# S5 data through DRAM in fewer transfers, and attention scores of meta and band keys in one product

## What is computed

```python
u = rmsnorm(h)                       # (528, 1024)
gla = gated_linear_attention(q, k, v, a)                 # chunks of 64, state passed on
y   = s5(u_s)                        # per group of 16 channels one 64-dim complex diagonal state
y   = gelu(y + d_skip * u_s); y = y * sigmoid(y @ w_glu)
s   = q @ keys.T + rel_bias          # keys: 16 meta, the chunk before, the own chunk
p   = exp(s - m) / (sum(exp(s - m)) + exp(sink - m))     # a sink per head
att = p @ vals
h   = h + merge(gates(u), gla, y, att) @ w_out
```

## Time and profile before

| | |
|---|---|
| median of 3 runs | 1917.71 us (1917.54 to 1918.06) |
| the profiled execution, its own time | 1920.78 us |
| its span, first to last instruction | 1919.0 us |
| TensorE busy, mean granted clock | 93%, 0.96 |
| weight loads of TensorE busy | 83% |
| DVE, ACT, POOL busy | 51%, 36%, 41% |
| DMA: moved, mean rate | 221.78 MB, 116 GB/s |

### The profile page before, as it was taken

One profiled execution on the slowest core, in us unless ns is written; L12 is line 12 of the kernel. 1 busy time (PEld: TensorE's weight loads), 2 busy tenths in 40 slices (PEclk: granted clock), 3 DMA queues, 4 the chain that ended last, 5 costly groups with the idle time before them and its releaser, 6 DMA issues.

```text
span 1919.0 us, 29485 instructions
## 1 busy us (share of the span) xinstructions
PE 1778.7 (93%) x12215; PEld 1592.5 (83%) x12215; DVE 969.2 (51%) x1527; ACT 693.9 (36%) x1236; POOL 791.1 (41%) x484
## 2 busy tenths in 40 slices
PE   6976899999998998999997999989999899999997
PEld 5876798999988998999996987777788688778886
DVE  8997125423428994277653222433334589634223
ACT  3443332443543222233333643333445222224232
POOL 2644566333223223433343786653333333244442
PEclk8898899999999998999998999999999999999999
DMA  8455236222254562535552333542222646333432
GB/s 147 136 162 154 76 91 133 73 77 69 65 139 135 181 178 78 105 93 168 170 155 73 110 88 92 114 115 73 66 67 64 191 167 208 90 91 96 144 100 87
DMA packets 357068, 221.78 MB, mean 116 GB/s; under 512 B 50628, under 2 KB 347768, under 8 KB 354376
## 3 DMA queue, kind: packets, MB, share of 16 engines
q1 hardware_dynamic: 346408, 189.75, 37.4%
q10 hardware_dynamic: 10528, 30.15, 4.6%
HBM read 172.17 MB, written 38.50 MB: 110 GB/s over the span
## 4 chain that ended last, share of the span: by engine, by line
PE 65%; DVE 10%; DMA 7%; POOL 7%; ACT 4%; SPq 4%; issue 3%; ACTq 0%; DVEq 0%; POOLq 0%
PE ring L807 47%; DMA sb_w_raw<-in_w_in 4%; POOL sb_w_lo L658 3%; PE ring L766 3%; PE aux L1066 2%; DVE sb_s_mat_prod L1553 2%; PE aux L1158 2%; DVE sb_s_prod L1553 2%; PE ring L788 1%; SPq L564 1%; PE aux L1145 1%; SPq L530 1%; DMA sb_w_raw<-in_w_s_out 1%; PE aux L1111 1%; DVE sb_s_rot L2052 1%
## 5 line engine op out<-in xcount | busy, mean ns | idle before, releaser
L658 POOL TENSOR_TENSOR sb_w_lo<-sb_w_raw,sb_w_hi 128x1024 fp32r<-128x1024 f32 x246 | 608.7, 2477 | 1044.3 <-ACT sb_w_hi L1210 1042.1
L1210 ACT ACTIVATE sb_w_hi<-sb_w_raw 128x1024 fp32r<-128x1024 f32 x246 | 260.1, 1057 | 618.0 <-DMA sb_w_raw<-in_w_in 359.7
L807 PE MATMUL ring<-sb_u_hi,sb_w_hi 128*128 128x264 f32 (+1 forms) x2112 | 366.8, 327 | 29.0 <-DVE sb_tmp_dve L1623 17.6
L807 PEld LDWEIGHTS ring<-sb_u_hi,sb_w_hi 128*128 128x128 f32 x2112 | 312.0, 201 | 61.5 <-DVE sb_tmp_dve L1623 19.3
L807 PE MATMUL ring<-sb_u_lo,sb_w_hi 128*128 128x264 f32 (+1 forms) x2112 | 338.4, 311 | 0.0
L807 PE MATMUL ring<-sb_u_hi,sb_w_lo 128*128 128x264 f32 (+1 forms) x2112 | 334.4, 309 | 0.0
L807 PEld LDWEIGHTS ring<-sb_u_lo,sb_w_hi 128*128 128x128 f32 x2112 | 298.4, 190 | 22.1
L807 PEld LDWEIGHTS ring<-sb_u_hi,sb_w_lo 128*128 128x128 f32 x2112 | 294.0, 188 | 21.0
L1242 ACT ACTIVATE sb_tmp_act<-ring 128x528 f32<-128x528 f32 (+1 forms) x112 | 67.4, 602 | 140.1 <-PE ring L807 131.8
L807 PE MATMUL ring<-sb_y_hi,sb_w_hi 128*128 128x264 f32 (+1 forms) x504 | 88.8, 326 | 3.4 <-ACT sb_w_hi L1210 3.4
L1473 ACT ACTIVATE sb_att_scores<-sb_att_scores,sb_att_neg_max 128x208 f32<-128x208 f32 x128 | 58.5, 458 | 91.5 <-DVE sb_att_neg_max L1841 91.5
(11 more groups left out here) (324 smaller groups left out, 2618.6 us busy)
## 6 DMA issues: line engine op xcount, KB each, us to landing
sb_w_raw<-in_w_in SPq DMA_DIRECT2D x166, 512.0 KB, 4.1
sb_s_loaded<-s_matrices ACTq DMA_DIRECT2D x16, 1808.0 KB, 7.5
s_matrices<-sb_s_phase SPq DMA_DIRECT2D x16, 528.0 KB, 3.2
s_matrices<-sb_s_mbt SPq DMA_DIRECT2D x16, 512.0 KB
s_matrices<-sb_s_ca SPq DMA_DIRECT2D x16, 512.0 KB
sb_w_raw<-in_w_gla_out SPq DMA_DIRECT2D x16, 512.0 KB, 4.1
sb_w_raw<-in_w_attn_out SPq DMA_DIRECT2D x16, 512.0 KB, 4.1
sb_w_raw<-in_s_w_glu SPq DMA_DIRECT2D x16, 512.0 KB, 3.9
```

The source lines that it names most:

```text
L658: pool.tensor_tensor(WL[:, w], WR[:, w], WH[:, w].bitcast(F32), ALU.subtract).then_inc(lo_ready, 1)
L807: last = pe.matmul(RING[:, 2 * r + hf, 0:c1 - c0], w[:, n % SLOTS, kt, :], moving(b[0], xx[:, kt], c0, c1), start=(term == 0 and kt == 0), ...
L1210: act.activation(WH[:, w], WR[:, w], ACT.Copy).then_inc(hi_ready, 1)
```

## The change

Two things. First, S5's input is written tile by tile to a DRAM tensor as soon as each `("sin", j)` block is evacuated, and read back at `("ag", 0)` by 4 transfers in place of 16; each output tile is written to a second DRAM tensor one block after it is made, and read back in three parts of 4 transfers each in place of 16. The last part's split moves from block 22 to block 23. Second, POOL copies the keys once per layer so that each window of meta and band keys lies contiguous, and the scores of a head pair are one product of 208 keys (144 for the first four units, which need no copy).

```diff
-S5_SPLIT = {21: ((0, 4), (4, 6)), 22: ((6, 8),)}
+S5_SPLIT = {21: ((0, 4), (4, 6)), 23: ((6, 8),)}
+SIN_OUT = {min(AT[("sin", j)] + 2, AT[("ag", 0)]): () for j in range(KT)}
+SIN_OUT = {at: tuple(j for j in range(KT) if min(AT[("sin", j)] + 2, AT[("ag", 0)]) == at) for at in SIN_OUT}
...
+        AKX = sb("att_k_windows", [P, 2, ATT_PAIRS - 1, BAND], at=r)
...
+        ZD = nc.dram_tensor("s5_in_rows", [DEPTH, KT, P, STRIDE, STEPS], F32).ap()
+        YD = nc.dram_tensor("s5_out_rows", [DEPTH, KT, P, QUADS, STEPS], F32).ap()
...
+                    if b in SIN_OUT:
+                        for j in SIN_OUT[b]:
+                            evacuated(sp, ly, ("sin", j))
+                            sp.dma_start(ZD[ly, j], Z[:, j]).then_inc(z_spilled, 16)
                     if name == ("ag", 0):
-
-                        evacuated(sp, ly, ("sin", 6), ("sin", 7))
                         sp.wait_ge(h_spilled, 16 * ly + 16)
                         sp.wait_ge(smax_ready, unit(ly, ATT_UNITS - 1))
-                    if name == ("ag", 0):
-                        for q in range(QUADS):
-                            for p in range(STRIDE):
-                                sp.dma_start(Z4[32 * p:32 * p + 32, :, q, :],
-                                             Z[32 * q:32 * q + 32, :, STRIDE - 1 - p, :]).then_inc(
-                                                 steps_loaded, 16)
+                        sp.wait_ge(z_spilled, 16 * KT * (ly + 1))
+                        for p in range(STRIDE):
+                            sp.dma_start(Z4[32 * p:32 * p + 32].rearrange("i j q c -> i (j q) c"),
+                                         ZD[ly, :, :, STRIDE - 1 - p, :].rearrange("j (q i) c -> i (j q) c", q=QUADS)
+                                         ).then_inc(steps_loaded, 16)
+                    if name in S5F and S5F.index(name) - 1 in S5_OUT:
+                        j = S5_OUT[S5F.index(name) - 1]
+                        aux_read(sp, ly, ("y", j))
+                        sp.dma_start(YD[ly, j], Z4[:, j]).then_inc(y_spilled, 16)
                     if name in S5F and S5F.index(name) in S5_YT:
                         j0, j1 = S5_YT[S5F.index(name)]
-                        aux_read(sp, ly, ("y", j1 - 2))
-                        aux_read(sp, ly, ("y", j1 - 1))
+                        sp.wait_ge(y_spilled, 16 * (KT * ly + j1))
                         for q in range(QUADS):
-                            for t in range(STRIDE):
-                                sp.dma_start(YZ[32 * q:32 * q + 32, j0:j1, t, :],
-                                             Z4[32 * t:32 * t + 32, j0:j1, q, :]
-                                             ).then_inc(yt_loaded[YT_PARTS.index((j0, j1))], 16)
+                            sp.dma_start(YZ[32 * q:32 * q + 32, j0:j1].rearrange("i j t c -> i (j t) c"),
+                                         YD[ly, j0:j1, :, q, :].rearrange("j (t i) c -> i (j t) c", t=STRIDE)
+                                         ).then_inc(yt_loaded[YT_PARTS.index((j0, j1))], 16)
...
+                    if b == AT[("av", 0)] + 3:
+                        pool.wait_ge(akd_loaded, 32 * ly + 32)
+                        pool.tensor_copy(AKX[:, :, :, 0:N_META],
+                                         AKD[:, :, 0:N_META].unsqueeze(2).broadcast_to([P, 2, ATT_PAIRS - 1, N_META])
+                                         ).then_inc(windows_ready, 1)
+                        for p in range(1, ATT_PAIRS):
+                            k0 = N_META + P * p - CHUNK
+                            pool.tensor_copy(AKX[:, :, p - 1, N_META:BAND], AKD[:, :, k0:k0 + 3 * CHUNK]
+                                             ).then_inc(windows_ready, 1)
...
-                    k0, nk = (N_META, P) if p == 0 else (q0 - CHUNK, 3 * CHUNK)
                     h = aux_take(ly, ("sc", u))
+                    if p:
+                        pe.wait_ge(windows_ready, ATT_PAIRS * (ly + 1))
                     for h2 in range(2):
-                        for keys, col, n in ((k0, BAND - nk, nk), (0, 0, N_META)):
-                            for a in range(2):
-                                rows = slice(64 * a, 64 * a + 64)
-                                c0 = BAND * h2 + col
-                                last = pe.matmul(AX_[:, 2 * h + a, c0:c0 + n], AQ[rows, 2 * i + h2, q0:q0 + P],
-                                                 AKD[rows, i // 2, keys:keys + n], start=True, stop=True)
+                        for a in range(2):
+                            rows = slice(64 * a, 64 * a + 64)
+                            keys = AKX[rows, i // 2, p - 1, :] if p else AKD[rows, i // 2, 0:N_META + P]
+                            n = BAND if p else N_META + P
+                            last = pe.matmul(AX_[:, 2 * h + a, BAND * h2:BAND * h2 + n], AQ[rows, 2 * i + h2, q0:q0 + P],
+                                             keys, start=True, stop=True)
```

More of the change, by code:

```diff
@@ L615, in _ @@
                     if name == ("mg1", 3):
                         for part in yt_loaded:
-                            sp.wait_ge(part, 256 * ly + 256)
+                            sp.wait_ge(part, 64 * ly + 64)
                         produced(sp, ly, ("glu", KT - 1))
@@ L1138, in step_inputs @@
                     if j == 0:
[L1139 removed]
+                        pe.wait_ge(steps_loaded, 64 * ly + 64)
                     pe.wait_ge(mats_in[j % 2], 16 * (4 * ly + j // 2) + 16)
```

10 lines of the change are left out of this document (5 added, 5 removed).

## The result

| | before | changed |
|---|---|---|
| median | 1917.54 us (1910.10 to 1918.06, 5 runs) | 1901.89 us (1898.04 to 1905.55, 5 runs) |
| ratio | | 0.9926, 95% interval 0.9904 to 0.9947 |
| the profiled execution, its own time | 1920.78 us | 1898.04 us |
| its span | 1919.0 us | 1896.2 us |

The change gains 15.7 us, 0.7%. The forecast was 1888 us, a gain of 29.4: the sign was right, the size half as large, and 1901.9 lies above the range (1871 to 1898).

What follows compares the result with a forecast made beforehand. TensorE was taken to bound the kernel, with 65% of the chain of waits. Scores 13.4 us plus gap B and gap C 16 us made 29.4 us, from 1917.7 to 1888 us; range 1871 to 1898.

Steps and rivals of the forecast that it cites:

- the scores' term: Attention's score products: half the weight loads go, saving 0.42 us per unit, 13.4 us in all (ends 2.9 and 17.6).
- gap A: TensorE's idle time and slow clock at the S5 stage's start, 9.5 and 11.2 us; claimed to stay, gain 0.
- gap B: TensorE's wait for DVE's state of scan 7, late in S5; claimed to go, worth 16 us together with gap C.
- The copy of the keys: Four POOL copies per layer in attention, at most 4.4 us; claimed to cost nothing.
- SP's issues: SP's queue in S5: 4 issues, 2.8 us, per place instead of 16; the new spills' issues claimed to cost nothing.
- rival 1: gap A closes too, because the old gathers held the load back; about 19 us more go, 1869 us; 17%.
- rival 3: gap B or gap C gives way to a new wait; one staying in both layers costs 6 to 10 us; 18%.
- Gap C: TensorE's wait for POOL's low part of ("glu", 0)'s weights, 2.24 us; claimed to go, 16 us together with gap B.
- Rival 4: S5's gathers through DRAM crawl and the load of ("ag", 3) lands late; at 70 KB/us, 1926 us; 4%.

Runs made afterwards that it cites:

- e13: The kernel before without its products of 16 keys; executed once, only score units read: 0.85 us for a later unit, 0.65 for an early one.
- e9: The changed kernel with the gathers of tiles 0 to 5 put ahead of the load of ("ag", 2) in SP's queue; ratio 0.9898 to the kernel before.
- e10: As e9, and the first load of the S5 matrices issued ahead of block ("ag", 0); ratio 0.9885 to the kernel before.
- e11: The changed kernel with one more POOL wait, holding low parts of odd S5F blocks from the ninth until the running scan's state; ratio 0.9890 to the kernel before.
- e14: The kernel before with the new scores and e11's wait, S5's moves as before; ratio 0.9904 to the kernel before.
- e4: The changed kernel with S5's outputs moved as before (16 transfers per part, last split at block 22); ratio 0.9977 to the kernel before.
- e1: The kernel before with the scores' change alone (key copies included), S5's moves as before; ratio 0.9948 to the kernel before.
- e5: The changed kernel run again, with nothing altered; ratio 0.9932 to the kernel before.
- e8: The changed kernel with tiles 0 to 6 gathered before tile 7's spill and the first S5 matrices' load issued before ("ag", 0); ratio 0.9956 to the kernel before.
- e3: The changed kernel with S5's input moved as before (16 transfers from SBUF to SBUF); ratio 0.9922 to the kernel before.
- e12: The kernel before with each product of 16 keys issued twice; executed once, only score units read: 1.65 us for a later unit, 1.45 for an early one.

## Why the prediction was partly right

The measured time lies outside the range: the change is worth half of what I had forecast, because the scores' term was too large, gap A grew where I had put nothing, and gap B came back in another place.

**Scores.** Fewer products make the unit shorter, as forecast; the size was off: 9.7 us for 13.4. The failed step is "I take the narrow pairs as held to the pace of their loads". The rows allowed 0.14 to 0.60 us for the narrow pairs, and I chose near the top because a unit's length was 16 times 0.07. Removing them frees 0.35 (e13).

**The copy of the keys, SP's issues.** Nothing, as forecast: the scores alone give what the units give, and the weight loads between the spills leave on time.

**Gap A stays.** It stays, and grew by 6.8 us, past the end I gave (3 us). The failed step is that the gathers were "at most a tail" beside a collision called "untouched". In both kernels the matrices move only when the input is through, and the load lands only behind the matrices, so what delays the input delays the load. Two terms ahead of that were short. I took 3 us for the last spill, from the row of the 528 KB spills of another stage; it took 4.7, and 5.5 with the one before it, so that the gathers start 1.7 us ahead of `("ag", 0)`. And I took 2.1 to 2.6 us for each gather; the four moved in 11.8, 3 us each. By the clock of the kernel before, which reaches `("ag", 0)` 7.8 us later, 99% of their packets have started at 570.5 and the last one lands at 577.4, and not "near 566 to 569". The collision itself was read rightly, and rival 1, that the old transfers alone held the load back, is refuted by e9: with most of the gathers out of the way the landing is back at 9 us, not at 5. In e10, with the matrices early too, it is 7.

**Gap B goes.** It went, for the reason given, and came back as the same thing two scans sooner. The step that failed is "the load leaves on time, as for scans 1 to 4, which stop nobody". The step looked at when the loads are issued, and not at what shares the DMA engines with the one behind the first read back. This is rival 3, which I gave 18%, in a form that it did not name. It costs more than the 6 to 10 us given there: both layers' rest is 274.4 us in the changed kernel and 263.3 in e11, 11.1 less. e11 shows the cause, and e14 that it had nothing to do with S5's moves as such.

**Gap C goes.** Right, in both layers; e4 and e14, with 16 issues, still have it. The 16 us for B and C together were not far off: from e1, which has both, to e11, which has neither and no hit on scan 5, the rest of the stage falls from 276.8 to 263.3 us in both layers together, 13.5 us, of which 8.7 come with e14's gate.

**Rival 4.** The gathers do not crawl: the input moves at 191 GB/s through DRAM and at 194 from SBUF, and at 189 by both routes in layer 1. The Trainium skill, "DMA: Bandwidth & Descriptors", section Why small descriptors are slow (HBM only), had given me 15 to 20% more time for the route through DRAM, as an estimate; the traces do not show it. The growth of gap A is the later start.

The sum with the measured terms: 9.7 - 6.8 + 5.1 = 8.0 us, and 1.6 us in layer 0 for the slow clock inside `("glu", 0)`, which went with gap C (its first 18 pairs took 5.97 us, and take 4.37). The medians give 15.7 and, in e5, 13 (0.9932). One interval of 0.002 is 4 us, and the 5.1 would be 2.2 by e5's profile, so the 3 to 6 us between stay open.

## What to carry to other kernels

When a transfer is late, look first at what else the DMA engines move between its issue and its landing, before it and just behind it. If they are full all that time, fewer issues do not help; starting the other bytes sooner does (e9), unless that puts a spill and its wait ahead of the load (e8). Going back to the old route (e3) shortened the start, but the rate is the same by both; there the input's first issue goes out 6.4 us ahead of `("ag", 0)` again, and not 1.7. A busy share of 1 or more says that the engines are full, and only the GB/s beside it, over a stretch with one kind of transfer, say how fast they are. Where an engine's stretched operation is a matter of phase, as a low part beside a scan, closing the gap by moving another transfer can bring it back at another scan; one wait that fixes the order (e11, e14) removes it. And price a small product by leaving it out, since doubling it gives another number (e12, e13).

## What was not expected of the hardware

- While a load in packets of 14464 bytes moves, one in packets of 512 bytes issued 0.1 us before it advances packet for packet with it, and so by 14 GB/s of about 400 (before, 569 to 572; likewise in the changed kernel, e3 and e9).
- 528-byte packets move at 189 to 194 GB/s from SBUF and at 189 to 191 from DRAM.
- One issue of a 264 KB spill held SP's queue for 7.47 us while the DMA engines were full (e8). In the changed kernel the same issue holds it for 0.58 us.
- A 528 KB gather from DRAM lands after 5.2 to 17.6 us where the DMA engines are full; the old 132 KB transfers landed after 2.7 to 4.0, with as many bytes to move in all, but issued over 12.3 us and not over 4.7.
- A narrow pair of products costs 0.175 us where it stands between wide ones, and 0.225 behind another narrow pair (e12, e13).
- Two profiled executions of one program differ by 15.5 us in span (1896.2 and 1911.7), with most waits at the same places; in the second one scan more is hit.
